# Two decoder layers on one core: layer loop unrolled, mixing attention taken two heads at a time, sigmoids moved to ScalarE, probabilities scaled on GpSimd

## The reference, cut to what matters

```
h = rms_norm(x);  z = h @ w_in                     # split into head groups
A: latent attention: q, k from low-rank c_q, c_kv; 8 heads, causal softmax over 512 keys
B: mLSTM, 4 heads:   q, k = silu(conv4(...)); o gate: sigmoid(o_pre) * h
C: dilated sliding-window attention, 4 heads of 64 (three branches, one count mask)
x += rms_norm(concat(A, B, C) @ w_out)
x += rms_norm(cross_attention(rms_norm(x), rms_norm(mem)))   # 4 heads, 256 memory rows
x += rms_norm(swiglu(rms_norm(x)))                           # 2816 wide
```

## Time and profile before

| | us |
|---|---|
| median of 3 runs (1823.3 to 1828.65) | 1825.67 |
| the profiled execution's own time | 1825.33 |
| its span, first to last instruction | 1823.5 |
| PE busy / DVE / ACT / POOL | 1669.0 / 1046.6 / 675.2 / 565.9 |

### The profile page before, as it was taken

The page is one execution under the profiler, slowest core; times in us unless marked ns, Lnnn a source line. Parts: engine busy times, 40 slices in busy tenths (PEclk is TensorE's granted clock), DMA queues, the critical chain, the costliest instruction groups (busy, mean ns, idle before and its releaser), DMA issues.

```text
span 1823.5 us, 20537 instructions
## 1 busy us (share of the span) xinstructions
PE 1669.0 (92%) x7040; PEld 1267.5 (70%) x7040; DVE 1046.6 (57%) x1511; ACT 675.2 (37%) x1148; POOL 565.9 (31%) x240
## 2 busy tenths in 40 slices
PE   6998899889989999999689988998899899999994
PEld 5864457767667888888468554477677678888883
DVE  5968872752257776600378678727531678765003
ACT  5322674444443332222143216644343432332221
POOL 1000103562234454444300001036613434444442
PEclk9989999999999999999889889998999999999997
DMA  5210002341112332223023110033412123222221
GB/s 224 93 60 33 24 1 104 105 137 59 58 46 91 105 102 95 102 93 103 25 95 104 36 35 13 1 116 105 137 47 69 55 84 109 98 96 100 102 95 58
DMA packets 39099, 146.50 MB, mean 80 GB/s; under 512 B 4976, under 2 KB 4976, under 8 KB 38256
## 3 DMA queue, kind: packets, MB, share of 16 engines
q1 hardware_dynamic: 39024, 145.53, 23.3%
HBM read 143.41 MB, written 2.10 MB: 80 GB/s over the span
## 4 chain that ended last, share of the span: by engine, by line
PE 41%; DVE 5%; issue 2%; POOL 1%; ACT 1%; DVEq 0%; POOLq 0%; ACTq 0%
PE bank L552 11%; PE bank L554 11%; PE bank L553 11%; PE bank L753 2%; PE bank L747 1%; POOL w_lo L522 1%; PE bank L725 1%; DVE tn_x L1128 1%; PE bank L794 1%; PE bank L784 1%; PE bank L677 1%; PE bank L685 1%; DVE y_f L1163 0%; DVE o_gate L1326 0%; PE bank L597 0%
## 5 line engine op out<-in xcount | busy, mean ns | idle before, releaser
L522 POOL TENSOR_TENSOR w_lo<-raw,w_hi 128x1024 fp32r<-128x1024 f32 x212 | 518.8, 2455 | 1175.9 <-ACT w_hi L853 1175.9
L552 PE MATMUL bank<-h_hi,w_hi 128*128 128x512 f32 x1312 | 534.4, 407 | 68.0 <-DVE h_lo L1152 39.9
L553 PE MATMUL bank<-h_lo,w_hi 128*128 128x512 f32 x1312 | 520.2, 396 | 0.0
L554 PE MATMUL bank<-h_hi,w_lo 128*128 128x512 f32 x1312 | 519.3, 396 | 0.0
L853 ACT ACTIVATE w_hi<-raw 128x1024 fp32r<-128x1024 f32 x256 | 268.1, 1050 | 223.9 <-PE bank L554 223.7
L552 PEld LDWEIGHTS bank<-h_hi,w_hi 128*128 128x128 f32 x1312 | 252.3, 192 | 140.5 <-issue 55.6
L553 PEld LDWEIGHTS bank<-h_lo,w_hi 128*128 128x128 f32 x1312 | 252.8, 193 | 55.6 <-issue 3.9
L554 PEld LDWEIGHTS bank<-h_hi,w_lo 128*128 128x128 f32 x1312 | 252.1, 192 | 53.8
L1114 DVE TENSOR_TENSOR acc<-acc,sq 128x512 f32<-128x512 f32 x86 | 73.3, 852 | 322.4 <-ACT sq L865 320.7
L1477 DVE RECIPROCAL acc<-acc 128x512 f32<-128x512 f32 x44 | 147.5, 3353 | 1.5
L552 PE MATMUL bank<-a_hi,w_hi 128*128 128x512 f32 x352 | 138.7, 394 | 0.0
(11 more groups left out here) (185 smaller groups left out, 2205.1 us busy)
## 6 DMA issues: line engine op xcount, KB each, us to landing
raw<-w_in SPq DMA_DIRECT2D x248, 512.0 KB, 3.3
raw<-first_in SPq DMA_DIRECT2D x12, 512.0 KB, 3.5
mem<-mem_in SPq DMA_DIRECT2D x3, 1024.0 KB, 4.9
x<-x_in SPq DMA_DIRECT2D x1, 2048.0 KB, 10.6
out<-x SPq DMA_DIRECT2D x1, 2048.0 KB, 6.3
consts<-c_in SPq DMA_DIRECT2D x1, 1728.0 KB, 14.3
gains<-g_in SPq DMA_DIRECT2D x2, 36.0 KB, 3.7
first_g<-first_g_in SPq DMA_DIRECT2D x3, 4.0 KB, 3.1
```

Source lines behind the costliest of these rows:

```text
L522: pool.tensor_tensor(w_lo[:, s, :], raw[:, s, :], w_hi[:, s, :].bitcast(F32), ALU.subtract).then_inc(split_lo, 1)
L552: pe.matmul(out_ap, l_hi, r_hi, start=start, stop=False)
L553: pe.matmul(out_ap, l_hi, r_lo, start=False, stop=False)
L554: return pe.matmul(out_ap, l_lo, r_hi, start=False, stop=stop)
```

## The change

- **Layers unrolled.** `nc.Fori(0, DEPTH)` becomes a Python loop in each engine's stream; no barrier, no clearing of semaphores: every wait counts on through `count(s, layer, n)`. The last `residual` of layer 0 issues layer 1's first `scaled_lo` and `add_square` between its own steps, ACT reads x as it is updated, and ACT, POOL and SP prepare units 0 to 3 of layer 1 while layer 0 ends. Gains of both layers are loaded once.
- **Start and end.** x is loaded in 4 pieces between the first 4 units; `mem` is loaded later, and its square and sum come in layer 0 after input tile HEAD + 1. x is stored in 4 pieces as it is updated.
- **Input projections.** The first HEAD = 3 tiles go k by k; `in` uses 6 banks (IN_BANKS) instead of 2. Before the token-major values PE waits until the last `in` tile is emptied. The latent norms' squares are summed by PE (`latent_sum`) instead of DVE adds. POOL makes `w_lo` of units 0 to 3.
- **Sigmoids on ACT.** exp(-ln(1 + exp(-x))): three ACT instructions with waits between them; DVE keeps one product per `silu`, `output_gate` is gone.
- **Mixing attention by pairs.** 24 steps of two units (heads 2p and 2p+1, same query block); lag 2 steps, 6 probability buffers. POOL does the 48 scalings. The two heads' outputs go to partitions 0 to 63 and 64 to 127 of one bank; one `h_hi` and one `h_lo` [128, 512] per pair.
- **Residual adds** are all on DVE. The cross-attention is as it was.

```diff
+                    for layer in range(DEPTH): ...        # in each engine's stream, was: nc.Fori(0, DEPTH)
...
                     def conv_exponential(j):
-                        act.wait_ge(conv_done, j + 1)
-                        act.activation(conv_in[:, j % 2, 3:3 + SEQ], ml_qk[:, j, :], ACT.Exp, scale=-1.0)\
-                           .then_inc(conv_exp, 1)
+                        act.wait_ge(conv_done, count(conv_done, layer, j + 1))
+                        e = conv_in[:, j % 2, 3:3 + SEQ]
+                        done(act.activation(e, ml_qk[:, j, :], ACT.Exp, scale=-1.0), act_step)
+                        done(act.activation(e, e, ACT.Ln, bias=one[:, :]), act_step)
+                        act.activation(e, e, ACT.Exp, scale=-1.0).then_inc(conv_exp, 1)
...
+                        if n == U_OUT + RING - 1:          # POOL, before it makes w_lo of unit 25
+                            for u in range(2 * PAIR_STEPS):
+                                w = causal_len(u // 2 % TB)
+                                pool.wait_ge(mix_at["inverted"], count(mix_at["inverted"], layer, u + 1))
+                                pool.tensor_scalar(pair_probs(u)[:, 0:w], pair_probs(u)[:, 0:w], stat[:, 2, u:u + 1],
+                                                   None, ALU.mult).then_inc(mix_at["probs"], 1)
...
+                    def pair_scores(s):                    # PE
+                        qb, n = s % TB, causal_len(s % TB)
+                        for i in range(2):
+                            u = 2 * s + i
...
+                            if u >= 4:
+                                pe.wait_ge(mix_at["masked"], count(mix_at["masked"], layer, u - 3))
+                            hd = mix_head(pair_unit(u)[0])
+                            pe.matmul(score_ring[u % 4][:, 0:n], hd["q"][:, qb * P:n], hd["k"][:, 0:n], start=True,
+                                      stop=True).then_inc(mix_at["scored"], 1)
+                    def pair_out(pair):
...
                         for kb in range(TB):
+                            for i in range(2):
+                                mm = pe.matmul(outs[pair % 2][64 * i:64 * i + 64, kb * P:SEQ],
+                                               mix_head(2 * pair + i)["v"](kb), pt_mix[:, i, kb, kb * P:SEQ],
+                                               start=(kb == 0), stop=(kb == TB - 1))
                         mm.then_inc(mix_at["out"], 1)
+                    for s in range(PAIR_STEPS + PAIR_LAG + 1):
+                        if s < PAIR_STEPS:
+                            pair_scores(s)
+                        t = s - PAIR_LAG
+                        if t >= 1 and t % TB == 0:
+                            pair_out(t // TB - 1)
+                        if 0 <= t < PAIR_STEPS:
+                            pair_transposes(t)
...
+                    for s in range(PAIR_STEPS + PAIR_LAG + 2):     # DVE
+                        if s < PAIR_STEPS:
+                            pair_mask(s)
+                        if 1 <= s <= PAIR_STEPS:
+                            pair_invert(s - 1)
+                        t = s - PAIR_LAG - 1
+                        if t >= 1 and t % TB == 0:
+                            pair_lo(t // TB - 1)
```

More of the change, by code:

```diff
@@ L197 @@
 POST = ("mix_post", "x_post", "ffn_post")
+LATENT = ("q", "kv")
 LATE_RMS = ("mix_pre", "ffn_pre")
 def squares_before(name):
[L204 removed]
+    return sum(k for n, k in NORMS[:NORM_AT[name]] if n not in LATENT)
 def normed_before(name):
@@ L224, in scaled_before @@
     return sum(k for n, k in NORMS[:NORM_AT[name]] if n in POST)
[L227 to L240, removed]
+N_SQUARES = sum(k for n, k in NORMS if n not in LATENT)
@@ L412, in counter, with dense_bank @@
             return done
+        def dense_bank(name, use):
+            return bank[use % IN_BANKS] if name == "in" else dense[use % 2]
         def c_tile(m):
@@ L454, in _, with make_lo @@
[L454 to L476, removed]
+                def make_lo(u):
+                    pool.wait_ge(split_hi, u + 1)
+                    pool.tensor_tensor(w_lo[:, u % RING, :], raw[:, u % RING, :], w_hi[:, u % RING, :].bitcast(F32),
+                                       ALU.subtract).then_inc(split_lo, 1)
@@ L550, in three @@
+                pe.wait_ge(fixed_set, 2)
+                for layer in range(DEPTH):
                     def three(out_ap, l_hi, l_lo, r_hi, r_lo, start, stop):
@@ L598, in norm_sum, with latent_sum @@
                           .then_inc(norm_summed, 1)
+                    def latent_sum(name, first, n):
+                        pe.wait_ge(latent_squared, count(latent_squared, layer, first + n))
+                        pe.wait_ge(ln_done, count(ln_done, layer, NORM_AT[name]))
+                        for k in range(n):
+                            mm = pe.matmul(norm_bank[:, :], const(C_ONES), sq[:, k, :], start=(k == 0),
+                                           stop=(k == n - 1))
+                        mm.then_inc(norm_summed, 1)
@@ L1013, in attention, with pair_hi @@
                                    .then_inc(a["exped"], 1)
-                    def mix_hi(head):
-                        hd = mix_head(head)
-                        act.wait_ge(mix_at["out"], head + 1)
-                        act.activation(h_hi[hd["row"]:hd["row"] + 64, hd["tile"], :], outs[head % 2][0:64, :],
-                                       ACT.Copy).then_inc(mix_at["out_hi"], 1)
-                    attention(mix_at, MIX_HEADS, p_mix, pt_mix, causal_len, 1, mix_hi)
+                    def pair_hi(pair):
+                        act.wait_ge(mix_at["out"], count(mix_at["out"], layer, pair + 1))
+                        act.activation(h_hi[:, mix_head(2 * pair)["tile"], :], outs[pair % 2][:, :], ACT.Copy)\
+                           .then_inc(mix_at["out_hi"], 1)
```

805 lines of the change are left out of this document (421 added, 384 removed).

## The result

The changed kernel takes 1817.03 us (median of 8 runs, 1813.68 to 1819.78), the kernel before 1826.87 (8 runs, 1823.3 to 1830.38): ratio 0.9947, 95% interval 0.9933 to 0.9960. It is faster by 0.5%; forecast was 3.6%, 1760 us. The profiled execution took 1816.6 us with a span of 1814.5, 9.0 less than the span before.

The account below looks back on a forecast made before the run. PE, busy 92% of the span, was taken to bound the kernel. Turn -15, end -7, start -1, input projections +3.6, mLSTM -16, mixing attention -31, elsewhere +1 sum to -65.4 from 1825.3: 1760 us, range 1736 to 1802.

Parts of the forecast that it names:

- start: Start of the kernel up to the third tile: 1 us saved, bounds -4 to +4.
- turn: Passage from layer 0 to layer 1 without barrier, reload and clearing: 15 us saved, DVE's chain bounding instead.
- end: End of the kernel, x stored in pieces: 7 us saved, bounds 4 to 8.
- Input projections: Input projections of both layers: 3.6 us lost to one more matmul and a wait for DVE per layer.
- mLSTM: mLSTM stages: 16 us saved, 8 a layer, from reciprocals leaving DVE, shorter `w_ml` waits and less time at low clock.
- Side-by-side output: Mixing attention: a pair's two output products run beside each other, so its output costs 2.3 us and not 4.6.
- PE's share: Mixing attention: PE's work per pair of causal heads falls from 11.5 to 9.2 us.
- rival A: Mixing attention: nothing runs side by side, only 1.6 of the 31 us gain remain, 1789 us; chance 0.22.
- The price of scaling in the latency loop: Mixing attention: scaling priced at 0.7 us in a DVE, POOL and PE loop of 8.0 us a pair; 9.5 taken.
- Rival B: Mixing attention: the loop through DVE and POOL bounds, 10.9 us a pair, 1777 us in all; chance 0.2.
- Rival C: Mixing attention drops to 1.2 GHz, 114 us instead of 79.4, about 1860 us, slower than before; chance 0.04.
- Elsewhere: After cross-attention, adds moved from POOL to DVE: half a microsecond lost a layer, +1 us in all.

Follow-up runs that it names:

- e4: The changed kernel with the mixing attention head by head as in the kernel before, scaling on DVE; 1792.81 us.
- e10: Changed kernel with lag three, scaling split between DVE and POOL, plus the output gate's sigmoid partly back on DVE; 1782.3 us.
- e2: The changed kernel without any scaling of the mixing attention's probabilities, reciprocals kept; 1760.83 us.
- e8: Like e2, without scaling, but the pair's eight output matmuls go head by head instead of alternating; 1784.48 us.
- e1: The changed kernel with the scaling of the mixing attention's probabilities back on DVE, lag still two steps; 1786.35 us.
- e5: The changed kernel, scaling still on POOL, with transposes three steps behind the scores instead of two; 1774.07 us.
- e6: The changed kernel with scaling on DVE and transposes three steps behind the scores instead of two; 1770.79 us.

## Why the prediction was wrong

- **Direction, start, turn, end: right.** The turn gave 15.6 for 13.2 (DVE's chain let PE start 4.5 us after the residual, 5 were said), the end 8.2 for 7, the start nothing, as said. The third tile came 18.4 us sooner, over the 17 called the best; 2.8 of it went again in the rest of the projections.
- **Input projections and mLSTM: right.** e4 gives 33 us for all but the attention, forecast 34.4; e10 gives 15 to 17.6 for the sigmoids of the output gate, forecast 16.
- **Side-by-side output and PE's share: right.** 9.59 us a pair without scaling (e2) for 9.2, the eight products in 2.37 us for 2.3; rival A is refuted by the trace and by e8.
- **The price of scaling in the latency loop: the step that failed.** The prediction saw the loop and wrote "Two steps of this loop take 2.4 + 1.6, thus 8.0 a pair", and took 9.5. Its two laps a pair held 1.4 us of scaling (0.7 a lap), 2.6 of masks, 0.8 of reciprocals and signals, 3.2 of PE work, and 1.5 of the output that was not to hide. The trace has, in the same order, 5.60, 1.69, 0.25, 3.22 and 2.30, together 13.06. So one term was wrong by far: it priced the scaling of one head per lap, where both heads' scalings stand one behind the other in POOL's queue, and on the wide steps the next step's two behind them before PE can go on. That is 4.2 us too little, and the output, none of which hides, 0.8; masks and signals were priced 1.5 too high. e1 puts a cheaper scaling into the same loop (11.37), e2 takes it out (9.59), e5 leaves POOL's scaling as it is and gives the lap a third step (9.88). One sum also has a slip without weight: 56 and 7.2 are 63.2, not 63.5.
- **Rival B was the right mechanism with too low a price**: 10.9 a pair, said to hold 0.2 of the chance, with the scaling at POOL's upper rate (which is where it was: 1.56 of 1.64 us) and no part of the output hidden. It too counted one head's scaling a lap, some 2 us a pair for 5.60, and came 2.2 us a pair short.
- **Rival C** (granted clock) came in part: 0.83 to 0.85 in the stage, of which 0.92 up to the fourth pair's output of layer 1 (0.93 up to the third of layer 2) and 0.75 from there to the end of the stage, where the longest waits of PE for POOL, 1.6 to 2.5 us, stand. By an estimate from the first layer's rows it cost some 4 us a layer, not 35: 13.8 and 14.0 us for the last two periods behind 12.8 for the one before, and 4.53 us for the last output group in place of 2.37 (as in e5, so that this part does not come from the slow loop alone).
- **Elsewhere**: +3.7 for +1. The 528 matmuls of the down projection follow each other in 0.2333 us on average for 0.2289, with no wait in either trace, 2.3 us a layer; the stage takes 456.5 to 457.9 us in every kernel built on the change, 455 before. What they read did not change. The memory map did (the gains of both layers are now resident), and so did the program around them (the layers are unrolled). No run separates these; the cause is open.

What the time is made of, then: of the 57 us missing 50 are the attention, of which e5 gives back 41 by one step of lag alone (177.4 us of attention in both layers, 136.4 in e5).

## What to carry to other kernels

When work of several engines is regrouped into larger steps, write down the lap (every instruction from one engine's wait round to the same wait, in queue order, with signals, and with all units of a step, not one) and divide by the number of steps that the lag covers; that number stands beside the sums of busy time, and the largest bounds. A helper engine two to three times slower costs 3 us, within the noise, where the lag covers it (e5 against e6) and 31 where it does not (the change against e1), with the same busy time. If an engine both waits and is waited for, try more lag before you move work.

A wait at the seam of two stages is a chain looking for a place: moving the instruction that is waited for moves the wait (4.0, 5.4, 6.5 us here) unless the chain gets shorter.

## What the runs showed of the hardware

- Two f32 products of 64 output rows in different halves of one bank, issued in turn, take 2.37 us for eight, as long as four alone; issued head by head 3.93.
- POOL's multiplication by a value per row costs 0.60 us for 128 and 1.56 for 512 columns, 0.32 us for every 128 columns more, where DVE takes 0.28 to 0.29 and 0.49. The Trainium skill, Trainium Architecture — The Big Picture, § The five engines, in one table, says that POOL streams elementwise work "2× slower than DVE"; here it is 2.1 times at 128 columns and 3.2 times at 512.
- For the heads of 64 contraction rows the two scores of a step, which lie in different rows of the array and go to different banks, also ran together: 1.13 us for both at 512 columns, 1.12 for one head's before. The first line is of the kernel after, the second of the kernel before; a product is two records.
```profile
1153.70 1.13 PE L741 MATMUL bank<-sw_qk 64*128 64x512 f32 x4
```
```profile
1158.71 1.12 PE L747 MATMUL bank<-sw_qk 64*128 64x512 f32 x2
```
